# Two 64-feature heads side by side in the value product of a fused attention kernel

## The chip, the cores and the metric

The kernel runs on one core of a Trainium2 chip. The metric is the device time of one execution in microseconds. The engines named below are TensorE (PE; PEld is its weight load), VectorE (DVE), ScalarE (ACT), GpSimd (POOL) and SyncE (SP), which issues the loads. The matmul results land in eight PSUM banks of 128 partitions x 512 f32, bank 0 to bank 7.

## The reference

Two blocks over 256 tokens of 1024 features are computed one after the other. The change lies in the first, `first_block`: in layer 0 eight "moba" heads and eight "fox" heads, in layer 1 four "diff" heads and eight sliding-window ("swa") heads, all but diff with 64 features.

```python
proj = h @ w_in_ab[j]                                     # layer 0
qa, ka, va, ga, qb, kb_, vb_, gb, fb = split_cols(proj, AB_SIZES)
qa, ka = rmsnorm(to_heads(qa, 8), ..), rmsnorm(to_heads(ka, 8), ..)
ya = from_heads(moba_attention(qa, ka, to_heads(va, 8), moba_slopes))
yb = from_heads(fox_attention(qb, kb_, to_heads(vb_, 8), log_f))
y = concatenate([ya * silu(ga), yb * silu(gb)], -1)
x = x + y @ w_out_ab[j]
# every head:  p = softmax(masked scores);  out = p @ v        (256 x 256) @ (256 x 64)
# layer 1 likewise with yc (diff), yd (swa): y = concatenate([yc * silu(gc), yd * silu(gd)], -1)
```

The second block (latent attention, cross-attention over a memory, two MLPs, stick-breaking attention) is not touched, but the kernel begins its memory projection ("mem part") inside the first block.

## The kernel before, in words

Each projection is done to f32 accuracy as three fp32r products (`three`, L498 to L500: high weights by high input, low by high, high by low). Weights stream from memory in units of 128 x 2048, which ScalarE casts to `w_hi` (L1425) and VectorE splits to `w_lo` (L1970), two instructions each for a unit. TensorE takes its work in the order in which the code issues it, and so does every other engine; between engines there are only semaphores. A bank may be written again when its last reader has signalled `readN`.

The attention of the first block is written as pairs of heads with projection work as filling (`pairs`). For pair p TensorE does: the scores of heads 2p and 2p+1 (`scores`, L640, banks 4 and 5), then twice, for the heads of the pair before: the transposes of the probabilities (`turn_probs`, L654, three 128 x 128 blocks in bank 6, the mask leaves the fourth out), a fill (a projection unit or part, given by a table with the fill's number), and the values (`values`, L666, bank 7). VectorE makes the logits and their row maxima (`logits`, L2188), ScalarE the exponentials and their sums (`exps`, L1588), ScalarE copies the transposed probabilities to SBUF (`turned_probs`, L1599), and VectorE takes the reciprocal of the sums (L2204) and multiplies the values by it and by the gate, which is already in SBUF as `arena` (`outputs`, L2213).

The values have the transposed probabilities as weights and the 64 columns of v as the moving side: three f32 matmuls a head, which the trace shows as six instructions of 64 columns. The result has tokens on partitions. The output projection wants features there, so the gated values are transposed on TensorE (`gated`, L552, eight 128 x 128 blocks for eight heads), cast by ScalarE to the high part (L1474) and subtracted by VectorE for the low part (L2026).

The gates silu(ga), silu(gb), silu(gd) come from VectorE (`gate_panel`, L2165), which reads the banks of the gate's projection and so frees them. On GpSimd only small work runs in this stage, the position and forget tables (L2711, L2714, L2717).

Of the kernel before, what the change touches and what calls it, by code (L numbers as in the profile page):

```python
# [21 lines left out]
ALU = mybir.AluOpType  # L22
# [6 lines left out]
P = 128  # L29
D = 1024  # L30
S = 256
# [163 lines left out]
def build(nc, A, out):  # L195
# [7 lines left out]
    with ExitStack() as ctx:  # L203
# [76 lines left out]
        norm_ready = sem("norm_ready")  # L280
# [112 lines left out]
        for k in heads:  # L393
            first_map = k["kind"] == "diff" and k["c"] == 0
            turns += not first_map
            outputs += k["kind"] in ("moba", "fox", "swa") or k["kind"] == "diff" and k["c"] == 1
            norms += k["kind"] in ("mla", "xa") or k["kind"] == "diff" and k["c"] == 1
            k.update(turn=turns, output=outputs, norm=norms)
# [57 lines left out]
        GATE_PARTS = ((0, 2, 4, 3), (2, 1, 5, 5), (3, 1, 6, 7))  # L456
# [5 lines left out]
        def _(pe):  # L462
# [180 lines left out]
            def turn_probs(k):  # L643
# [3 lines left out]
                if k["kind"] in ("moba", "fox", "swa", "sb"):  # L647
                    pe.wait_ge(probs_ready, g + 1)
                else:
                    pe.wait_ge(norm_ready, k["norm"])  # L650
# [6 lines left out]
            def values(k):  # L657
# [10 lines left out]
                end(("Y", g), ins, (y_ready, k["output"]))  # L668

# [199 lines left out]
            def pairs(ks, fill):  # L869

                for p in range(len(ks) // 2 + 1):
                    if 2 * p < len(ks):
                        scores(*ks[2 * p:2 * p + 2])
                    for n in range(2):
                        old = ks[2 * p - 2 + n] if p else None
                        if p:
                            turn_probs(old)
                        for f in fill.get(2 * p + n, []):
                            f()
                        if p:  # L880
                            values(old)

            def gated(name, panel, b0, need, first=0, chunks=4):

                return transposes(name, lambda t, c: arena[:, panel, t * PANEL + (first + c) * P:t * PANEL + (first + c + 1) * P],
                                  chunks, lambda t: (y_ready, need), b0)
# [6 lines left out]
            def gate_part(key, panel, n, ks):  # L893

                first, chunks, b0, last = GATE_PARTS[n]
                yr[key, n] = gated((key, n), panel, b0, ks[last]["output"], first, chunks)

            def gate_chunk(key):
# [11 lines left out]
                0: [unit("qb", 0)], 1: [unit("qb", 1)], 2: [unit("kb", 0)], 3: [unit("kb", 1), turn("qb", 4, 1)], 4: [lambda: row_scales(("n", 0), 1), lambda: fgate(r)],  # L910
                5: [unit("vb", 0), turn("kb", 5, 1)], 6: [lambda: tok_unit("vb", 1, decay_cols)], 7: [unit("gb", 0)], 8: [lambda: turn_mem(0, 0, 2), unit("gb", 1)],
                9: [lambda: turn_mem(0, 1, 2)], 10: [mem_part(0, 0)], 11: [mem_part(0, 1)], 12: [lambda: gate("yab0", 3, 0, heads_of("moba")[-1]["output"])],
                13: [mem_part(1, 0)], 14: [mem_part(1, 1)], 15: [half("oab", 0, "yab0", 0)],
                16: [half("oab", 0, "yab0", 1), lambda: gate_part("yab1", 7, 0, heads_of("fox"))],
                17: [half("oab", 1, "yab0", 0), lambda: gate_part("yab1", 7, 1, heads_of("fox"))]})
            half("oab", 1, "yab0", 1)()
            gate_part("yab1", 7, 2, heads_of("fox"))
# [12 lines left out]
            for i in range(5):  # L930
# [13 lines left out]
                0: [mem_part(2, 1), lambda: gate("ycd0", 3, (0, 3), heads_of("diff")[-1]["output"])], 2: [mem_part(3, 0)], 3: [mem_part(3, 1)],  # L944
                4: [half("ocd", 0, "ycd0", 0)], 5: [half("ocd", 0, "ycd0", 1)], 6: [half("ocd", 1, "ycd0", 0, (0, 1))], 7: [half("ocd", 1, "ycd0", 0, (2, 3))],
                8: [half("ocd", 1, "ycd0", 1, (0,)), lambda: gate_part("ycd1", 6, 0, heads_of("swa"))],
                9: [half("ocd", 1, "ycd0", 1, (1,)), lambda: gate_part("ycd1", 6, 1, heads_of("swa"))]})
            half("ocd", 1, "ycd0", 1, (2, 3))()
            gate_part("ycd1", 6, 2, heads_of("swa"))
# [423 lines left out]
        def read_of(name):  # L1373
# [3 lines left out]
        panel_of = {"qa": 0, "ka": 1, "va": 2, "ga": 3, "qb": 4, "kb": 5, "vb": 6, "gb": 7,  # L1377
                    "qc": 0, "kc": 1, "vc": 2, "gc": 3, "qd": 4, "kvd": 5, "gd": 6}

# [35 lines left out]
        def _(act):  # L1415
# [48 lines left out]
            def hi_one(name, c, dst, base=0, in_bank=2):  # L1464
# [10 lines left out]
                own.sig(ins, hiT_ready)  # L1475

# [187 lines left out]
            def pairs(ks, units_at, after, ahead={}, both_turned=()):  # L1664

                for p in range(len(ks) // 2 + 1):
                    for n in range(2):
                        i = 2 * p + n
                        if p and i - 1 not in both_turned:
                            turned_probs(ks[i - 2])  # L1670
                        if i in both_turned:
                            turned_probs(ks[i - 1])
# [15 lines left out]
            def mem_unit(i, n):  # L1688
# [14 lines left out]
                11: (("xkv", 0, 0), 0), 13: (("xkv", 0, 1), 0), 15: ("oab", 0, 0), 17: ("oab", 1, 0)}, {  # L1703
                0: [lambda: gate_finish("ga")], 1: [qk_squares("qb")], 2: [qk_rsqrt("qb")],
# [4 lines left out]
                12: [lambda: hi_T("yab0", 4, xT_hi)], 14: [lambda: mem_unit(0, 1)],  # L1709
                16: [lambda: hi_T(("yab1", 0), 2, xT_hi, 4)], 17: [lambda: hi_T(("yab1", 1), 1, xT_hi, 6)]},  # L1710
                {9: [lambda: hi_T(("m", 0, 1), 4, hT_hi, 4)], 10: [lambda: gate_finish("gb")]})
            hi_T(("yab1", 2), 1, xT_hi, 7)
# [24 lines left out]
            for i in range(4 + 2):  # L1737
# [22 lines left out]
                for f in extra.get(i, []):  # L1760
                    f()
            pairs(heads_of("swa"), {2: ("gd", 1), 3: (("xkv", 0, 2), 0), 5: (("xkv", 0, 3), 0)},
                  {1: [lambda: hi_T("ycd0", 4, xT_hi)],
                   8: [lambda: hi_T(("ycd1", 0), 2, xT_hi, 4)], 9: [lambda: hi_T(("ycd1", 1), 1, xT_hi, 6)]},
                  {4: [lambda: mem_unit(0, 2), lambda: mem_unit(0, 3)]}, (6,))
            hi_T(("ycd1", 2), 1, xT_hi, 7)
# [194 lines left out]
        def _(dve):  # L1961
# [236 lines left out]
            def recip(k):  # L2198
# [5 lines left out]
                link(V.reciprocal(rsum[:, 2 * g:2 * g + 2], e))  # L2204

            def outputs(k):

                recip(k)
                g, vd = k["g"], k["vd"]
                ps = condition(dve, ("Y", g))  # L2210
# [633 lines left out]
```

## Time and profile before

| quantity | value |
| --- | --- |
| median of 3 runs | 951.78 us (950.68 to 952.01) |
| profiled execution | 951.7 us |
| its span, first to last instruction | 949.9 us |
| TensorE busy | 936.1 us (99%) |
| VectorE busy | 637.9 us (67%) |
| ScalarE busy | 544.1 us (57%) |
| GpSimd busy | 57.2 us (6%) |

The span is what the trace covers; the execution is 1.8 us longer, and the durations below are of the span. The stage of moba and fox lies about at 58 to 157 us, that of swa at 256 to 289 us. In a timeline row "x6" means that six like instructions that follow each other are one row, and its duration is that of the whole row; TensorE's rows overlap by their pipeline, so what a group costs there is the distance from its start to the next start.

### The profile page before, as it was taken

The numbers are of one execution on the slowest core, as the hardware profiler recorded it, in microseconds if no ns is written. First come the engines' busy times: TensorE is split into PE (matmuls) and PEld (weight loads), VectorE is DVE, ScalarE is ACT, GpSimd is POOL, SyncE is SP. The second block draws the span as 40 slices with busy tenths as digits, with TensorE's granted clock in tenths as the row PEclk, the third lists the DMA queues.
The fourth block names the chain that finished last, engine by engine and source line by source line (L and its number), as shares of the span: only waits on it lengthen the run. The fifth ranks groups of instructions, "written<-read, shape, count | busy, mean of one in ns | idle before, by whom it ended". The sixth has DMA issues, their size and how long they took to land.

```text
span 949.9 us, 14440 instructions
## 1 busy us (share of the span) xinstructions
PE 936.1 (99%) x5452; PEld 815.5 (86%) x5452; DVE 637.9 (67%) x1258; ACT 544.1 (57%) x1046; POOL 57.2 (6%) x109
## 2 busy tenths in 40 slices
PE   9999999999999999999999999999999999999997
PEld 7778788888888898989888888899988898888886
DVE  4888784877776667667666656477964767556664
ACT  6686673657676575567444444465754666444442
POOL 3001330002010030000000000000000000000000
PEclk9999999999999999999999999999999999999999
DMA  9986534554334274445556656665455256655641
GB/s 286 260 194 121 175 133 158 181 181 146 136 121 113 77 211 161 149 130 173 187 179 198 200 177 233 183 184 153 139 173 177 89 178 189 204 183 179 201 175 44
DMA packets 109584, 159.88 MB, mean 168 GB/s; under 512 B 10734, under 2 KB 45900, under 8 KB 109260
## 3 DMA queue, kind: packets, MB, share of 16 engines
q1 hardware_dynamic: 109080, 158.40, 53.7%
q8 instruction: 44, 0.72, 0.3%
q10 hardware_dynamic: 436, 0.56, 0.2%
q14 instruction: 24, 0.20, 0.1%
HBM read 156.32 MB, written 2.11 MB: 167 GB/s over the span
## 4 chain that ended last, share of the span: by engine, by line
PE 92%; DVE 3%; ACT 1%; issue 1%; DMA 1%; SPq 1%; DVEq 0%; ACTq 0%
PE bank L498 22%; PE bank L500 22%; PE bank L499 22%; PE bank L1206 9%; PE bank L1209 5%; PE bank L640 3%; PE bank L654 2%; PE bank L666 2%; PE bank L552 2%; DVE w_lo L1970 1%; DMA raw<-in_w_in_ab 1%; PE bank L625 1%; PE bank L1347 1%; SPq L2759 1%; DVE xT L2028 0%
## 5 line engine op out<-in xcount | busy, mean ns | idle before, releaser
L1970 DVE TENSOR_TENSOR w_lo<-raw,w_hi 128x1024 fp32r<-128x1024 f32 (+3 forms) x296 | 335.2, 1177 | 136.6 <-ACT w_hi L1425 136.1
L1425 ACT CAST w_hi<-raw 128x1024 fp32r<-128x1024 f32 (+3 forms) x296 | 282.1, 1011 | 128.2 <-DMA raw<-in_mlp_w_in 72.0
L498 PE MATMUL bank<-w_hi,xT 128*128 128x512 f32 (+1 forms) x366 | 145.2, 397 | 1.4 <-issue 0.9
L500 PE MATMUL bank<-w_hi,xT 128*128 128x512 f32 (+1 forms) x366 | 141.2, 386 | 0.0
L499 PE MATMUL bank<-w_lo,xT 128*128 128x512 f32 (+1 forms) x366 | 140.9, 385 | 0.0
L498 PE MATMUL bank<-w_hi,hT_hi 128*128 128x512 f32 (+1 forms) x348 | 136.7, 393 | 2.0 <-DVE w_lo L1970 1.7
L500 PE MATMUL bank<-w_hi,hT_lo 128*128 128x512 f32 (+1 forms) x348 | 135.0, 388 | 0.0
L499 PE MATMUL bank<-w_lo,hT_hi 128*128 128x512 f32 (+1 forms) x348 | 134.9, 388 | 0.0
L498 PE MATMUL bank<-xT,w_hi 128*128 128x256 f32 x368 | 106.0, 288 | 0.3 <-DVE w_lo L1970 0.3
L1206 PE MATMUL bank<-xT,w_hi 128*128 128x512 f32 x384 | 104.5, 394 | 0.0
L500 PE MATMUL bank<-xT,w_lo 128*128 128x256 f32 x368 | 104.1, 283 | 0.0
L499 PE MATMUL bank<-xT,w_hi 128*128 128x256 f32 x368 | 104.0, 283 | 0.0
L498 PEld LDWEIGHTS bank<-w_hi,xT 128*128 128x128 f32 x366 | 68.8, 188 | 15.5 <-DVE w_lo L1970 2.0
L500 PEld LDWEIGHTS bank<-w_hi,xT 128*128 128x128 f32 x366 | 68.7, 188 | 14.3
L499 PEld LDWEIGHTS bank<-w_lo,xT 128*128 128x128 f32 x366 | 69.0, 188 | 12.3
L498 PEld LDWEIGHTS bank<-w_hi,hT_hi 128*128 128x128 f32 x348 | 65.4, 188 | 16.1 <-DVE w_lo L1970 1.9
L500 PEld LDWEIGHTS bank<-w_hi,hT_lo 128*128 128x128 f32 x348 | 65.3, 188 | 13.6
L499 PEld LDWEIGHTS bank<-w_lo,hT_hi 128*128 128x128 f32 x348 | 65.4, 188 | 12.4
L1206 PEld LDWEIGHTS bank<-xT,w_hi 128*128 128x128 f32 x384 | 66.5, 189 | 9.6
L498 PEld LDWEIGHTS bank<-xT,w_hi 128*128 128x128 f32 x368 | 70.5, 191 | 1.5 <-issue 0.7
L499 PEld LDWEIGHTS bank<-xT,w_hi 128*128 128x128 f32 x368 | 70.5, 192 | 0.3
L500 PEld LDWEIGHTS bank<-xT,w_lo 128*128 128x128 f32 x368 | 70.5, 191 | 0.0
(276 smaller groups left out, 1313.7 us busy)
## 6 DMA issues: line engine op xcount, KB each, us to landing
raw<-in_mlp_w_in SPq DMA_DIRECT2D x32, 1024.0 KB, 5.2
raw<-in_mlp_w_out SPq DMA_DIRECT2D x32, 1024.0 KB, 5.1
raw<-in_w_in_ab SPq DMA_DIRECT2D x13, 1024.0 KB, 10.6
raw<-in_w_in_cd SPq DMA_DIRECT2D x13, 1024.0 KB, 5.1
raw<-in_xa_w_kv SPq DMA_DIRECT2D x8, 1024.0 KB, 5.1
raw<-in_sb_w_qkv SPq DMA_DIRECT2D x16, 512.0 KB, 5.0
raw<-in_w_out_ab SPq DMA_DIRECT2D x4, 1024.0 KB, 5.2
raw<-in_w_out_cd SPq DMA_DIRECT2D x4, 1024.0 KB, 5.1
```

What stands on the lines that cost most here:

```text
L498: pe.matmul(o, wh, ih, start=start, stop=False, skip_group_check=True)
L499: pe.matmul(o, wh, il, start=False, stop=False, skip_group_check=True)
L500: return pe.matmul(o, wl, ih, start=False, stop=stop, skip_group_check=True)
L552: ins = pe.transpose(o, src(t, c), ident[:, :])
L625: ins = pe.transpose(o, arena[:, panel, t * w + c * P:t * w + (c + 1) * P], ident[:, :])
L640: ins = pe.matmul(o[:, a:z], q(t * P, (t + 1) * P), kk(0, z - a), start=n == 0, stop=n == len(k["parts"]) - 1)
L654: ins = pe.transpose(banks[b][:, n * P:(n + 1) * P], src[:, a:a + P], ident[:, :])
L666: ins = pe.matmul(banks[b][:, t * vd:(t + 1) * vd], k["pt"][:, n * P:(n + 1) * P], k["v"](kt), start=m == 0, stop=m == len(mine) - 1)
L1206: pe.matmul(banks[b][:, :], wh[c], xT[:, k].rearrange("p a s -> p (a s)"), start=k == 0, stop=False, skip_group_check=True)
L1209: ins = pe.matmul(banks[b][:, 0:S], wl[c], xT_hi[:, k, :], start=False, stop=k == KC - 1, skip_group_check=True)
L1425: nc.scalar.copy(w_hi[:, u % SLOTS, a], raw[:, u % SLOTS, a]).then_inc(hi_ready, 1)
L1970: V.tensor_tensor(w_lo[:, u % SLOTS, a], raw[:, u % SLOTS, a], w_hi[:, u % SLOTS, a].bitcast(F32), ALU.subtract).then_inc(lo_ready, 1)
```

## The change

The probabilities are divided by their sum before they are transposed, not the values after. For moba this is done by GpSimd (`scale_probs`, two instructions a head, signal `divided`), for fox and swa by VectorE (`normalise`, which the kernel already had for other heads: a reciprocal and two instructions a head, signal `norm_ready`). The values are then done for two heads at once, at the end of the pair: v is the weight (64 columns), the transposed probabilities move, and the two heads stand in the column halves of the array and in the partition halves of bank 7 (`values_pair`). The result has features on partitions, so the output needs no transposes. Instead the gates are transposed (`turn_gate`, eight blocks a gate, into two banks; ScalarE copies the first back to SBUF, VectorE the second), and one VectorE instruction a pair multiplies values by gate (`outputs`). The high and low parts are then made from SBUF (`gated_hi`, `gated_lo`). In the tables of the fills some parts move: the memory parts 1 from 13 and 14 to 12 and 13, the halves of the output projection "oab" from 15 to 17 to 14 to 17, and ScalarE's and VectorE's casts with them.

```diff
 # TensorE
+            def values_pair(ka, kb):
+                begin(("Y", g), 7)
+                pe.wait_ge(probsT_ready, kb["turn"])
+                places = ((ka, 0), (kb, HD))
+                for k, a in places:
+                    pe.matmul(banks[7][a:a + HD, 0:S], k["v"](0), k["pt"][:, 0:S], start=True, stop=False, tile_position=(0, a), ...)
+                for k, a in places:
+                    ins = pe.matmul(banks[7][a:a + HD, P:S], k["v"](1), k["pt"][:, S:S + P], start=False, stop=True, tile_position=(0, a), ...)
+            def turn_gate(name, bs):
+                for t in range(T):
+                    for one in released[name, t]:
+                        pe.wait_ge(*one)
+                for n, b in enumerate(bs):
+                    begin(("gT", name, n), b)
...
+                            ins = pe.transpose(o, arena[:, panel, t * PANEL + c * P:t * PANEL + (c + 1) * P], ident[:, :])
 # pairs, TensorE
                     for n in range(2):
-                        old = ks[2 * p - 2 + n] if p else None
                         if p:
-                            turn_probs(old)
+                            turn_probs(ks[2 * p - 2 + n])
                         for f in fill.get(2 * p + n, []):
                             f()
-                        if p:
-                            values(old)
+                    if p:
+                        values_pair(*ks[2 * p - 2:2 * p])
-                1: [unit("qb", 1)],
+                1: [unit("qb", 1), lambda: turn_gate("ga", (3, 7))],
-                11: [mem_part(0, 1)],
+                11: [mem_part(0, 1), lambda: turn_gate("gb", (0, 1))],
 # swa
-                3: [mem_part(3, 1)],
+                3: [lambda: turn_gate("gd", (0, 3)), mem_part(3, 1)],
 # ScalarE
-                2: [qk_rsqrt("qb")],
+                2: [qk_rsqrt("qb"), lambda: turned_gate("ga")],
-                12: [lambda: hi_T("yab0", 4, xT_hi)], 14: [lambda: mem_unit(0, 1)],
+                12: [..., lambda: turned_gate("gb"), lambda: gated_hi("moba", range(4), 0)],
+                13: [lambda: mem_unit(0, 1)],
 # VectorE
             def outputs(k):
-                recip(k)
...
-                    ins = V.scalar_tensor_tensor(out=o, in0=ps[:, t * vd:(t + 1) * vd], scalar=rsum[...], in1=o, op0=ALU.mult, op1=ALU.mult)
+                own.sig(V.tensor_tensor(o, ps[:, 0:S], o, ALU.mult), gated_ready)
+                        if 2 * p < len(ks) and ks[2 * p]["kind"] == "moba":
+                            recip(ks[2 * p + n], inverted)
+                        elif 2 * p < len(ks):
+                            normalise(ks[2 * p + n])
+                1: [lambda: turned_gate("ga")],
 # GpSimd
+            def scale_probs(k):
+                pool.wait_ge(inverted, g + 1)
+                for t, (a, z) in enumerate(k["spans"]):
+                    ins = G.tensor_scalar(o, o, rsum[:, 2 * g + t:2 * g + t + 1], None, ALU.mult)
+                if n in (3, 5, 7, 9):
+                    scale_probs(heads[n - 3])
+                    scale_probs(heads[n - 2])
```

Three places show how the order changes; each has the rows of the kernel before first. The first is TensorE, after the fill 1 (unit qb 1 into banks 0 and 1), at the scores of heads 2 and 3. "ident" is the identity of the transposes.

```order
L640 MATMUL bank4<-arena 128x128 [waits qkT_ready,logits_ready]
L640 MATMUL bank4<-arena 128x256
L640 MATMUL bank5<-arena 128x128
L640 MATMUL bank5<-arena 128x256
L654 MATMUL bank6<-ident,pb3 128x128 [waits probs_ready,qkT_ready]
L654 MATMUL bank6<-ident,pb3 128x128 x2
L498 MATMUL bank2<-w_hi,xT 128x512 [waits loT_ready,read2,lo_ready]
```

In the changed kernel TensorE has at the same place:

```order
L703 MATMUL bank3<-ident,arena 128x128 [waits read3,read2]
L703 MATMUL bank3<-ident,arena 128x128 x3
L703 MATMUL bank7<-ident,arena 128x128 [waits qkT_ready]
L703 MATMUL bank7<-ident,arena 128x128 x3
L645 MATMUL bank4<-arena 128x128 [waits qkT_ready,logits_ready]
L645 MATMUL bank4<-arena 128x256
L645 MATMUL bank5<-arena 128x128
L645 MATMUL bank5<-arena 128x256
L661 MATMUL bank6<-ident,pb3 128x128 [waits divided,qkT_ready]
L661 MATMUL bank6<-ident,pb3 128x128 x2
L503 MATMUL bank2<-w_hi,xT 128x512 [waits loT_ready,read2,lo_ready]
```

The gate's eight transposes stand ahead of the scores and wait for both halves of gate_panel ga (`read3,read2`, VectorE's L2165). The next rows are the unit kb 0: twelve matmuls into bank 2, then twelve into bank 3. In both kernels the first into bank 3 waits for `read3`; in the kernel before VectorE's L2165 gives it, now ScalarE's copy of the transposed gate. That copy is here, on ScalarE, at head 2; in the kernel before ScalarE has there:

```order
L1588 ACTIVATE pb3,esum<-nl3,nmax 128x128 [waits written6,logits_ready]
L1588 ACTIVATE pb3,esum<-nl3,nmax 128x256
L1425 CAST w_hi<-raw 128x1024 [waits w_in3]
L1425 CAST w_hi<-raw 128x1024
L1460 ACTIVATE lnv<-var 128x16 [waits var_ready]
L1462 ACTIVATE guess<-lnv 128x16 [waits act_chain]
L1599 COPY pt3<-bank6 128x384 [waits written6]
```

And in the changed one:

```order
L1634 ACTIVATE pb3,esum<-nl3,nmax 128x128 [waits written6,logits_ready]
L1634 ACTIVATE pb3,esum<-nl3,nmax 128x256
L1458 CAST w_hi<-raw 128x1024 [waits w_in3]
L1458 CAST w_hi<-raw 128x1024
L1493 ACTIVATE lnv<-var 128x16 [waits var_ready]
L1495 ACTIVATE guess<-lnv 128x16 [waits act_chain]
L1514 COPY arena<-bank3 128x512 [waits written3,written7]
L1645 COPY pt3<-bank6 128x384 [waits written6]
```

The copy (L1514) stands behind the exponentials of head 2, the casts of the next weight unit and two small instructions, and ahead of the copy of head 1's probabilities. The third place is ScalarE at head 12; in the kernel before, with the copies of the probabilities of heads 10 and 11 as first and last row:

```order
L1599 COPY pt3<-bank6 128x384 [waits written7,written6]
L1588 ACTIVATE pb3,esum<-nl3,nmax 128x128 [waits written6,logits_ready]
L1588 ACTIVATE pb3,esum<-nl3,nmax 128x256
L1474 CAST xT<-bank0 128x256 [waits written0] x2
L1474 CAST xT<-bank1 128x256 [waits written1] x2
L1599 COPY pt3<-bank6 128x384 [waits written7,written6]
```

In the changed kernel, between the same two copies:

```order
L1645 COPY pt3<-bank6 128x384 [waits written7,written6]
L1634 ACTIVATE pb3,esum<-nl3,nmax 128x128 [waits written6,logits_ready]
L1634 ACTIVATE pb3,esum<-nl3,nmax 128x256
L1458 CAST w_hi<-raw 128x1024 [waits w_in0]
L1458 CAST w_hi<-raw 128x1024
L1514 COPY arena<-bank0 128x512 [waits written0,written1,units_used]
L1521 CAST xT<-arena 128x256 [waits gated_ready] x4
L1645 COPY pt3<-bank6 128x384 [waits written7,written6]
```

In the kernel before the casts of the next weight unit come behind head 13; now they and the copy of the transposed gate gb (bank 0) stand at head 12, ahead of the four high parts and of the copy of head 11's probabilities, for which the values of the pair (10, 11) wait.

## Rows read from the trace of the kernel before

**Rows 1.** The page: busy time of each engine, and granted TensorE clock in 40 slices.

```profile
PE 936.1 (99%) x5452; PEld 815.5 (86%) x5452; DVE 637.9 (67%) x1258; ACT 544.1 (57%) x1046; POOL 57.2 (6%) x109
...
PEclk9999999999999999999999999999999999999999
```

**Rows 2.** TensorE, timeline: start us, us, engine, line, op, out<-in, count [idle before].

```profile
67.57 0.93 PE L640 MATMUL bank<-arena 64*128 64x128 f32 x8
68.44 0.55 PE L654 MATMUL bank<-ident,pb 128*128 128x128 f32 x3
68.74 0.47 PE L498 MATMUL bank<-w_hi,xT 128*128 128x512 f32 x1
74.29 0.78 PE L666 MATMUL bank<-arena,pt 128*128 128x64 f32 x6
```

**Rows 3.** VectorE and ScalarE, timeline of the same stretch.

```profile
67.71 1.41 DVE L2165 SCALAR_TENSOR_TENSOR arena<-bank,rstd,xn 128x512 f32<-128x512 f32 x2 [0.27 <-ACT xn L1575]
69.59 2.36 DVE L1970 TENSOR_TENSOR w_lo<-raw,w_hi 128x1024 fp32r<-128x1024 f32 x2 [0.47 <-ACT w_hi L1425]
73.39 0.28 DVE L2188 CUSTOM_DVE_ANT_0 nl<-bank,alibi 128x128 f32<-128x128 f32 x1
74.07 0.40 ACT L1588 ACTIVATE pb<-nl,nmax 128x128 f32<-128x128 f32 x1 [2.29 <-DVE nmax L2188]
74.96 1.98 ACT L1425 CAST w_hi<-raw 128x1024 fp32r<-128x1024 f32 x2
```

**Rows 4.** Groups by form: line, engine, op, shapes, count, busy us, mean ns, idle before.

```profile
L666 PE MATMUL bank<-arena,pt 128*128 128x64 f32 x144 | 18.9, 267 | 1.3 <-DVE arena L2213 1.1 <-ACT pt L1599 0.2
L2222 DVE TENSOR_SCALAR pb<-pb,rsum 128x256 f32<-128x256 f32 x8 | 2.8, 349 | 0.0
L2044 DVE COPY mem<-bank 128x512 f32<-128x512 f32 x4 | 2.7, 682 | 0.0
L1696 ACT COPY mem<-bank 128x512 f32<-128x512 f32 x8 | 4.5, 583 | 0.2 <-PE bank L500 0.2
```

**Rows 5.** GpSimd, one group by form.

```profile
L2711 POOL TENSOR_SCALAR alibi<-arena,small 128x256 f32<-128x256 f32 x8 | 7.4, 924 | 0.0
```

**Rows 6.** TensorE, timeline of the cross-attention values.

```profile
406.11 0.60 PE L676 MATMUL bank<-arena,mem 128*128 128x256 f32 x2
406.54 0.59 PE L677 MATMUL bank<-arena,mem 128*128 128x256 f32 x2
```

**Rows 7.** TensorE, timeline around the fox heads' middle.

```profile
126.00 0.88 PE L666 MATMUL bank<-arena,pt 128*128 128x64 f32 x6 [1.08 <-DVE arena L2213]
126.98 0.36 PE L498 MATMUL bank<-hT_hi,w_hi 128*128 128x256 f32 x1
129.93 0.78 PE L666 MATMUL bank<-arena,pt 128*128 128x64 f32 x6
130.64 0.93 PE L640 MATMUL bank<-arena 64*128 64x128 f32 x8
```

**Rows 8.** VectorE and ScalarE, timeline of the same stretch.

```profile
125.28 0.16 DVE L2204 RECIPROCAL rsum<-esum 128x2 f32<-128x2 f32 x1
131.21 2.56 DVE L1970 TENSOR_TENSOR w_lo<-raw,w_hi 128x1024 fp32r<-128x1024 f32 x2
133.69 0.28 DVE L2188 CUSTOM_DVE_ANT_0 nl<-bank,alibi 128x128 f32<-128x128 f32 x1
130.12 1.99 ACT L1425 CAST w_hi<-raw 128x1024 fp32r<-128x1024 f32 x2
135.25 1.17 ACT L1474 CAST xT<-bank 128x256 fp32r<-128x256 f32 x4
136.30 0.51 ACT L1599 COPY pt<-bank 128x384 f32<-128x384 f32 x1
```

**Rows 9.** TensorE and ScalarE, timeline of the sliding-window heads.

```profile
268.90 1.98 ACT L1425 CAST w_hi<-raw 128x1024 fp32r<-128x1024 f32 x2
270.11 0.48 PE L498 MATMUL bank<-w_hi,xT 128*128 128x512 f32 x1
```

More of the change, by code:

```diff
@@ L395, in build @@
             turns += not first_map
-            outputs += k["kind"] in ("moba", "fox", "swa") or k["kind"] == "diff" and k["c"] == 1
-            norms += k["kind"] in ("mla", "xa") or k["kind"] == "diff" and k["c"] == 1
+            outputs += k["kind"] == "diff" and k["c"] == 1
+            norms += k["kind"] in ("fox", "swa", "mla", "xa") or k["kind"] == "diff" and k["c"] == 1
             k.update(turn=turns, output=outputs, norm=norms)
@@ L646, in turn_probs @@
                 begin(("PT", g), b)
-                if k["kind"] in ("moba", "fox", "swa", "sb"):
+                if k["kind"] == "sb":
                     pe.wait_ge(probs_ready, g + 1)
+                elif k["kind"] == "moba":
+                    pe.wait_ge(divided, g + 1)
                 else:
@@ L891, in gate, with gate_chunks @@
                 yr[key] = gated(key, *a)
-            def gate_part(key, panel, n, ks):
-                first, chunks, b0, last = GATE_PARTS[n]
-                yr[key, n] = gated((key, n), panel, b0, ks[last]["output"], first, chunks)
+            def gate_chunks(key, chunks):
+                yr[key] = chunks_ready(state["loT"])
+                state["loT"] += chunks
             def gate_chunk(key):
@@ L1475, in hi_one, with turned_gate, gated_hi @@
                 own.sig(ins, hiT_ready)
+            def turned_gate(name):
+                condition(act, ("gT", name, 1))
+                ps = condition(act, ("gT", name, 0))
+                nc.scalar.copy(pan(panel_of[name], 0), ps[:, :]).then_inc(read_of(("gT", name, 0))[0], 1)
+                own.last = read_of(("gT", name, 0))
+            def gated_hi(kind, ps, base):
+                for p in ps:
+                    act.wait_ge(gated_ready, pair_no[kind] + p + 1)
+                    own.sig(nc.scalar.copy(xT_hi[:, base + p, :], gated_chunk(kind, p)), hiT_ready)
             def hi_T(name, chunks, dst, base=0):
@@ L1662, in _, with pairs @@
             front("qa", "ka", "va", "ga")
-            def pairs(ks, units_at, after, ahead={}, both_turned=()):
+            def pairs(ks, units_at, after, ahead={}):
                 for p in range(len(ks) // 2 + 1):
@@ L2203, in recip, with turned_gate, gated_lo @@
                     link(V.tensor_tensor(e, e, col(ESINK + 2 * k["h"], 2), ALU.add))
-                link(V.reciprocal(rsum[:, 2 * g:2 * g + 2], e))
-            def outputs(k):
-                recip(k)
-                g, vd = k["g"], k["vd"]
-                ps = condition(dve, ("Y", g))
-                for t in range(T):
-                    o = k["gate"](t)
-                    ins = V.scalar_tensor_tensor(out=o, in0=ps[:, t * vd:(t + 1) * vd], scalar=rsum[:, 2 * g + t:2 * g + t + 1],
-                                                 in1=o, op0=ALU.mult, op1=ALU.mult)
-                    own.sig(ins, y_ready if t == T - 1 else None)
+                link(V.reciprocal(rsum[:, 2 * g:2 * g + 2], e), s)
+            def turned_gate(name):
+                ps = condition(dve, ("gT", name, 1))
+                V.tensor_copy(pan(panel_of[name], 1), ps[:, :]).then_inc(read_of(("gT", name, 1))[0], 1)
+                own.last = read_of(("gT", name, 1))
+            def outputs(k):
+                o = gated_chunk(k["kind"], k["h"] // 2)
+                ps = condition(dve, ("Y", k["g"]))
+                dve.wait_ge(*read_of(("gT", {"moba": "ga", "fox": "gb", "swa": "gd"}[k["kind"]], k["h"] // 4)))
+                own.sig(V.tensor_tensor(o, ps[:, 0:S], o, ALU.mult), gated_ready)
+            def gated_lo(kind, ps, base):
+                for p in ps:
+                    dve.wait_ge(hiT_ready, lo_T[0] + 1)
+                    lo(xT_lo[:, base + p, :], gated_chunk(kind, p), xT_hi[:, base + p, :], None)
             def normalise(k):
@@ L2313, in _, with pairs @@
             front("qa", "ka", "va", "ga")
-            def pairs(ks, after, late, between={}, early=()):
+            def pairs(ks, after, late, between={}):
                 for p in range(len(ks) // 2 + 1):
```

103 lines of the change are left out of this document (60 added, 43 removed).

## The prediction

> **What bounds the kernel now.** I read the page first. TensorE is busy for 936.1 us of a span of 949.9 [rows 1], so a microsecond of TensorE work or waiting is a microsecond of time, and work on another engine costs only where TensorE waits for it. The granted clock is in the top tenth in all 40 slices [rows 1]. Then TensorE's groups by form, for the values and for what they wait [rows 4]: L666 with 64 columns is busy for 18.9 us in 144 instructions, with 1.3 us of idle time ahead of them, 1.1 of it behind VectorE's L2213. Last the timelines at three places where the order changes: fill 1 to 2 [rows 2, 3], heads 8 to 13 [rows 7, 8] and swa [rows 9]. There I replayed the changed order by hand, each instruction with the duration of its nearest row. The reader is to see that these stages run with hardly any idle TensorE, while ScalarE and VectorE are only just ahead.
>
> **The values.** Before, the six instructions of a head take from 129.93 to 130.64 when scores follow, 0.71 us [rows 7], and 0.6 ahead of the transposes, where no row-half mode begins; a pair is 1.32 (my rounding of both). The new pair has two matmuls of 256 and two of 128 columns. The nearest row is the scores L640: two heads side by side in row halves, the same columns, eight instructions, from 67.57 to 68.44 or 0.87 [rows 2]. I add 0.1 for the second mode change and take 0.95. Saving: 12 pairs x 0.37 = 4.4 us. The bounds come from the cross-attention values: two instructions of 256 columns start 0.43 apart from the next two [rows 6], so one f32 product of 256 columns is 0.43 and one of 128 half of it. If the column halves run fully side by side the pair is 0.43 + 0.22 = 0.65, and 12 pairs save 8.0. If they run one behind the other it is 1.30, with the same 0.3 of overhead as L640 has over 0.65 it is 1.6, and 12 pairs cost 3.4 more than before. I take L640's value because it has the same shapes. The Trainium skill, TensorEngine Tiling (Array Packing), Key Properties, says that different tiles can run in parallel and that a change of mode drains the engine. L640's 0.87 against 0.65 agrees with both for row halves; no row here shows column halves.
>
> **The transposes.** 24 of gated values go and 24 of gates come (8 for each of ga, gb, gd), the same blocks at about 0.1 each (three take 0.30 [rows 2]): nothing, but those of ga come early, where TensorE then waits anyway; I count them once, at nothing.
>
> **First wait: gate ga.** TensorE is free for the transposes at 67.57 [rows 2], but the gate's panel is written by L2165 from 67.71 to 69.12 [rows 3], which itself waited for ScalarE. Before, nobody on TensorE needed it until bank 2. Cost 69.12 - 67.57 = 1.55. Queued behind are the scores of heads 2 and 3, on which the whole chain of VectorE and ScalarE hangs, but VectorE is busy with w_lo until 71.95 (69.59 + 2.36), so that harms nobody else.
>
> **Second wait: bank 3.** TensorE then has transposes 0.8, scores 0.87, probabilities 0.30 and the twelve products into bank 2, half of 68.74 to 74.29, 2.78 [rows 2]: it is at bank 3 at 69.12 + 4.75 = 73.87. Bank 3 is now freed by ScalarE's copy, behind the exponentials and the casts. VectorE's logits of head 2 began at 73.39 [rows 3]; ahead of them now stand two reciprocals of 0.16 [rows 8] and the copy of bank 7, 0.68 [rows 4]: 1.0 later. Exponentials then at 74.07 + 1.0 = 75.07, done and cast begun 0.89 later at 75.96, cast 1.98 to 77.94 [rows 3], two small 128x16 instructions, by estimate 0.4, and the copy of 128x512, 0.58 [rows 4]: 78.9. The cost is 78.9 - 73.9 = 5.0. It is the largest term and nothing hides it: TensorE has no other work in its order. The 1.55 and 5.0 are 6.5 together. GpSimd's two instructions for head 0 (0.92 and somewhat less [rows 5]) stand ahead of bank 2's products; as TensorE comes 1.55 + 0.8 later than before, and 5 us of waiting follow, up to 5 us of lateness there cost nothing.
>
> **Heads 8 to 13.** Before values of head 8 TensorE waited until 126.00 for L2213, that is for VectorE behind a w_lo that ended at 125.28 [rows 7, 8]. Now the probabilities of head 9 wait for its normalising behind the same w_lo: 0.16 and twice up to 0.35 [rows 4, 8], to 126.1. One wait takes the place of the other: 0. New is the wait of pair (10, 11). Its scores (12, 13) begin 0.5 later than 130.64, with eight transposes of gb (0.8) more and the first values (0.6) less ahead of them and the pair's 0.24 over one head's values: 131.1. From there 0.87 + 0.3 + twice a memory part of 2.95 (126.98 to 129.93 [rows 7]) + 0.3 = 7.4, so TensorE is at the pair at 138.5. On ScalarE: the logits at 133.69 [rows 8] become 134.4 by the copy of bank 1 on VectorE (0.68), exponentials from 135.0 to 135.9, cast 1.9, copy 0.5 (0.58 less its overlap), four high parts 1.1 and the copy of head 11's probabilities 0.5 [rows 8]: 139.9. Cost 1.4. By the same kind of count, the last fox pair waits 0.6 for a copy behind a cast of 1.98 and two high parts (by estimate), and the wait of 0.2 behind L1599 [rows 4] goes.
>
> **Swa.** The first half of the output projection "ocd" begins at 270.11 [rows 9] and needs bank 0; it comes 0.8 later by the transposes of gd and 0.4 sooner by the pair. ScalarE frees the bank only behind the cast of 268.90, which lasts 1.98 and starts some 1.0 later, since VectorE normalises two heads (0.16 + twice up to 0.35 each, less what L2213 took) ahead of the logits: copy done at 268.9 + 1.0 + 1.9 + 0.5 = 272.3. Cost 1.8, less some 0.4 that the first pair has already lost waiting: 1.4 here and 0.4 there, 1.8 in all.
>
> **Sum.** -4.4 + 6.5 + 1.4 + 0.6 - 0.2 + 1.8 = +5.7 on an execution of 951.7, or 957.4. Two waits behind VectorE at about 103 and 121 us stay; TensorE comes later to them by the delay of the front, and I take 0.2 off: 957.2. The median of the runs is 0.1 above the profiled execution, which changes nothing.
>
> **The rivals.** (1) The column halves do not run side by side. For it: no row shows them; against it: the row halves do. A pair of 1.3 in place of 0.95 costs 4.2: 961.4. (2) The other side: the wait for bank 3 does not form, because ScalarE comes to the copy before TensorE comes to the bank; for that its chain would have to be 5.0 shorter, against what [rows 3] show. It decides alone: with the second wait gone the sum is +0.7, and with pairs of 0.65 it is -2.9, or 948.8. Partly for it: the bound of 0.65 is not excluded; but by itself it gives only 953.6. (3) GpSimd is the late one. Its instructions read SBUF, and so does w_lo on VectorE, from both operands. If each of the 16 instructions runs at twice the 0.92 [rows 5], a head takes up to 3.7 instead of 1.8; head 0 is covered, but for the three later pairs one wait of some 0.6 each is possible: 959.0. Against it: between the reciprocal and the transposes there are 2.8 us of a unit. The Trainium skill, SBUF — State Buffer, states a lock between the two engines' shared port, by which one waits for the other's whole instruction when VectorE has two SBUF inputs; a w_lo instruction lasts 1.18 here (2.36 for two [rows 3]), so by it head 0 would be 1.2 to 2.4 late, and the sum stays, since the wait for bank 3 covers that. (4) The granted clock falls after the 5 us without a matmul. The profile of before has no such idle stretch there, and never a lower clock [rows 1]; if the next 3 us of work ran at half speed it would cost some 3: 960.2.
>
> **How the numbers follow.** My forecast, with pairs of 0.65 to 1.1 and waits as worked out within 1.5 us: 0.62, on its own 953.5 to 959.5. Rival 1: 0.12. Rival 2, or a mixture of most of it with fewer of the later waits: 0.12. Rival 3: 0.06. Rival 4: 0.08. A range of 952.6 to 961.6 leaves out the far side of rival 2 and the edges of 1 and 4. A difference of under 0.2% (1.9 us) cannot be told from no change here. Faster takes most of rival 2, 0.07; same takes its rest and the low edge of the forecast, 0.07; slower is 0.86.
>
> **What would show it right or wrong.** TensorE idle for about 1.5 us ahead of the first L703 with VectorE's L2210 as releaser, and for about 5 us ahead of the thirteenth product of kb 0 (L503 into bank 3), with ScalarE's L1514 as releaser; from there all later instructions 7 us later than before, 0.8 of which comes back where the gated values were transposed. L684 and L687 of a pair 0.95 from start to start of the next group. TensorE waiting 1.4 us for L1645 ahead of the pair (10, 11), and for L1514 at the half "ocd". I am wrong if bank 3 comes free before 75 us, if the pairs cost 1.3 or more, or if a low granted clock stands behind the first long wait.

## The result and the profile after

The changed kernel takes 959.3 us (median of 5 runs, 958.73 to 959.58) against 951.17 us before (median of 5, 950.68 to 952.01): a ratio of 1.0081, interval 1.0069 to 1.0092. It is slower by 8 us. The forecast was 957.2, with a range of 952.6 to 961.6.

The page of the changed kernel, to stand against [rows 1]:

```profile
span 957.7 us, 14333 instructions
PE 933.9 (98%) x5404; PEld 806.1 (84%) x5404; DVE 644.8 (67%) x1257; ACT 546.3 (57%) x1049; POOL 76.1 (8%) x125
...
PEclk9999999999999999999999999999999999999999
```

TensorE has 2 us less work and the span is 7.8 longer, so about 10 us more waiting (the 2 us less hold a stretch of low clock, shown below). The tenths of the granted clock say nothing here: a dip of 3 us is too short for a slice of 24. The timeline of TensorE in the front of the stage answers to [rows 2]:

```profile
69.81 1.06 PE L703 MATMUL bank<-ident,arena 128*128 128x128 f32 x8 [1.96 <-DVE arena L2210]
73.39 0.52 PE L661 MATMUL bank<-ident,pb 128*128 128x128 f32 x3 [1.65 <-POOL pb L2760]
73.67 0.47 PE L503 MATMUL bank<-w_hi,xT 128*128 128x512 f32 x1
79.21 0.80 PE L503 MATMUL bank<-w_hi,xT 128*128 128x512 f32 x1 [2.53 <-ACT arena L1514]
```

There are three waits within ten microseconds where there was none: for VectorE's gate panel (1.96), for GpSimd's scaling of head 0 (1.65), and for ScalarE's copy that frees bank 3 (2.53). What stands behind them on the other engines answers to [rows 3]:

```profile
68.26 1.41 DVE L2210 SCALAR_TENSOR_TENSOR arena<-bank,rstd,xn 128x512 f32<-128x512 f32 x2 [0.26 <-ACT xn L1621]
70.14 2.41 DVE L2015 TENSOR_TENSOR w_lo<-raw,w_hi 128x1024 fp32r<-128x1024 f32 x2 [0.27 <-ACT w_hi L1458]
74.17 0.69 DVE L2254 COPY arena<-bank 128x512 f32<-128x512 f32 x1
74.78 0.28 DVE L2233 CUSTOM_DVE_ANT_0 nl<-bank,alibi 128x128 f32<-128x128 f32 x1
76.34 1.98 ACT L1458 CAST w_hi<-raw 128x1024 fp32r<-128x1024 f32 x2
78.59 0.57 ACT L1514 COPY arena<-bank 128x512 f32<-128x512 f32 x1
69.97 3.28 POOL L2760 TENSOR_SCALAR pb<-pb,rsum 128x128 f32<-128x128 f32 x2 [6.10 <-DVE rsum L2249]
74.23 1.50 POOL L2760 TENSOR_SCALAR pb<-pb,rsum 128x128 f32<-128x128 f32 x2 [0.98 <-DVE rsum L2249]
```

The chain predicted for ScalarE is there link by link: logits at 74.78 behind the copy of bank 7, exponentials at 75.45, cast at 76.34, copy at 78.59 (predicted 78.3 to 78.9), TensorE in bank 3 at 79.21. GpSimd's pair of instructions takes 3.28 us at 69.97, beside VectorE's w_lo, and 1.50 at 74.23, where VectorE works from PSUM. After the wait, windows of one microsecond on TensorE (busy, count, granted clock) show this:

```profile
79.00:80.00 1.00, 0.79 (x2) 0.58 0.00 0
80.00:81.00 1.00, 1.00 (x4) 0.50 0.00 0
82.00:83.00 1.00, 1.00 (x5) 0.71 0.00 0
83.00:84.00 1.00, 1.00 (x8) 1.00 0.00 0
```

The clock is at 0.50, the 1.2 GHz level, from 79.2 to 82.6; products then start 0.43 apart and not 0.23, which over these 3.4 us costs 1.7 (the expectations below put it at 1.8). Later waits, in the same columns as the timeline:

```profile
105.06 0.52 PE L661 MATMUL bank<-ident,pb 128*128 128x128 f32 x3 [0.89 <-ACT arena L1606]
134.58 0.52 PE L661 MATMUL bank<-ident,pb 128*128 128x128 f32 x3 [1.25 <-DVE pb L2275]
148.52 0.65 PE L684 MATMUL bank<-pt,arena 128*64 128x256 f32 x4 [1.47 <-ACT pt L1645]
161.39 0.65 PE L684 MATMUL bank<-pt,arena 128*64 128x256 f32 x4 [0.43 <-ACT pt L1645]
280.06 0.47 PE L503 MATMUL bank<-w_hi,xT 128*128 128x512 f32 x1 [1.18 <-DVE w_lo L2015]
279.38 0.58 ACT L1514 COPY arena<-bank 128x512 f32<-128x512 f32 x1
```

The old waits behind VectorE's decay work and the memory's transposes stay, at 112.47 and 130.22. At 280.06 the page names w_lo, but ScalarE's copy of the gate gd out of bank 0 ends at 279.96, 0.1 ahead of TensorE's start, so it is the bank. And this is the pair of values, whose start-to-start distance answers to the 1.32 of two heads before [rows 7]:

```profile
90.42 0.65 PE L684 MATMUL bank<-pt,arena 128*64 128x256 f32 x4
90.90 0.39 PE L687 MATMUL bank<-pt,arena 128*64 128x128 f32 x4
91.22 0.93 PE L645 MATMUL bank<-arena 64*128 64x128 f32 x8
```

From 90.42 to 91.22 it takes 0.80 us.

I added up TensorE's start-to-start distances by group over both traces. Idle time went from 5.5 to 15.5 us (+10.0); projections take 2.8 more, 1.7 of it the low clock; most of the rest is the last product ahead of each new wait, which counts with its whole 0.39 and not with the 0.23 to a next start; the values of the 24 heads went from 15.7 to 9.6 (-6.1); transposes and scores of all kinds +0.9; small rest +0.2. Together +7.8, the difference of the spans.

### The profile page after: what moved, and what is told of

Its sections match the earlier page's. It is cut to its first block, busy times and chain, and to the rows that moved or that the text cites. A ratio compares the mean times of both kernels' runs of the same rounds, so it can differ in the third digit from the quotient of the medians.

```text
span 957.7 us, 14333 instructions
## 1 busy us (share of the span) xinstructions
PE 933.9 (98%) x5404; PEld 806.1 (84%) x5404; DVE 644.8 (67%) x1257; ACT 546.3 (57%) x1049; POOL 76.1 (8%) x125
## 4 chain that ended last, share of the span: by engine, by line
PE 85%; DVE 6%; ACT 5%; issue 2%; DMA 1%; SPq 1%; DVEq 0%; ACTq 0%
PE bank L503 21%; PE bank L505 20%; PE bank L504 20%; PE bank L1242 9%; PE bank L1245 5%; PE bank L645 3%; ACT w_hi L1458 2%; DVE w_lo L2015 2%; PE bank L661 2%; PE bank L557 1%; ACT pb L1634 1%; DMA raw<-in_w_in_ab 1%; PE bank L1383 1%; DVE xT L2073 1%; PE bank L630 1%
```

## The experiments

Eleven kernels were run, each an edit of the changed kernel, in four groups with runs of the kernel before on the same chip (medians of before 951.42 us for a to d, 951.49 for e to h, 951.76 for i, 951.80 for j and k).

**a. Bank 3 freed early.** ScalarE's order at head 2:

```diff
-                2: [qk_rsqrt("qb"), lambda: turned_gate("ga")],
+                2: [qk_rsqrt("qb")],
...
+                {2: [lambda: turned_gate("ga")], 9: ...     # ahead of the exponentials
```

> ScalarE's copy of the transposed gate ga out of bank 3 is moved ahead of the exponentials of head 2. Theory (the bank is the cost): the copy ends at about 75.0 us, TensorE comes to bank 3 at 76.3, so the wait of 2.7 us goes, and with it the 3.4 us at half clock that followed (1.8 us): 959.3 - 4.5 = 954.8. Rival (the wait only moves): ScalarE's exponentials and casts are the limit of this stretch, TensorE waits for head 1's or 2's probabilities instead, and less than 1.5 us is gained: 958 or more.

Measured 954.13 us, ratio 1.0031 (1.0019 to 1.0042): 5.2 under the changed kernel, 0.7 more than expected. The wait for bank 3 is gone. The profiled execution, at 956.35 the slowest of its seven, has TensorE's first two waits at the same places (1.79 and 1.01) and the low clock from 70.2 to 77.0:

```profile
69.07 1.06 PE L703 MATMUL bank<-ident,arena 128*128 128x128 f32 x8 [1.79 <-DVE arena L2210]
72.66 0.87 PE L661 MATMUL bank<-ident,pb 128*128 128x128 f32 x3 [1.01 <-POOL pb L2760]
```

```profile
70.00:71.00 1.00, 1.00 (x9) 0.60 1.01 164
76.00:77.00 1.00, 1.00 (x4) 0.50 0.00 0
```

So the bank is the largest single cause, and the clock can also fall without it, behind the wait for the gate. The mean granted clock is 0.998 in the six other executions and 0.996 in all five of the changed kernel: the 5.2 holds most likely the 1.7 of the low clock as well as the wait.

**b. Moba on VectorE, nothing on GpSimd.** `norms` counts moba too, VectorE calls `normalise` for all heads, and `scale_probs` is gone.

> The moba heads are normalised on VectorE like the others, GpSimd scales nothing. Theory (ScalarE's late copy of bank 3 sets the front, GpSimd's lateness is covered by it): TensorE's wait for head 0's probabilities (1.7 us) goes, but VectorE's logits of head 2 come 1.3 us later by two normalisings of 0.64, the bank with them, so the wait there grows from 2.7 to 5.7; at about 105 us 1.0 is gained. Together about +0.3: 959.6. Rival (GpSimd is itself the cost): both waits for it go and nothing comes in their place, -2.7: 956.6.

Measured 959.22 us, ratio 1.0080 (1.0066 to 1.0094): no gain, as the theory said. The wait for GpSimd is gone, and the products into bank 3 begin 0.84 later than in the changed kernel (80.05 against 79.21):

```profile
70.02 1.92 PE L701 MATMUL bank<-ident,arena 128*128 128x128 f32 x8 [1.96 <-DVE arena L2208]
80.05 0.62 PE L503 MATMUL bank<-w_hi,xT 128*128 128x512 f32 x1 [3.27 <-ACT arena L1512]
```

The wait there is 3.27, not the 5.7 of the theory. A part of the difference is that TensorE came later: its clock was low from 70.0 to 73.5 already, and a second time from 80.3 to 83.7. The first of the two stretches lies ahead of the wait for the bank and is covered by it.

**c. TensorE kept busy ahead of bank 3.**

```diff
+                    if name == "kb" and n == 0 and (t, c) == (1, 0):
+                        keep_busy()          # 24 transposes of ident into bank 6
```

> 24 transposes of the identity into the free bank 6 are put ahead of the wait for bank 3 (extra work, no result is used); at 0.11 us each they fill 2.6 of the 2.7 us of waiting. Theory (the lower clock from 79.2 to 82.6 us comes from that idle time): the granted clock stays 1.00 and the 1.8 us go: 957.5. Rival (the clock falls for the waits before it, or whatever TensorE does there): 959.3 to 959.5, with the same stretch at 0.50.

Measured 957.76 us (956.68 to 959.48 in five), ratio 1.0067 (1.0055 to 1.0080). It does not settle the question: in the profiled execution (959.48) the low clock lies ahead of the filled stretch, from 70.6 to 77.4, behind the wait for the gate. Over the five runs the mean granted clock goes with the time: 0.995 in the two of 959.1 and 959.5, 0.998 to 0.999 in those of 956.7 to 957.8. But this doesn't price the clock alone, since the fill has a fixed length: in the profiled execution TensorE came late to it, and the 24 transposes ran from 78.34 to 80.88, past the 79.2 at which the bank had come free in the changed kernel. Nor is the fill shown to keep the clock up: d, whose order is that of the changed kernel up to its first values at 88.8, has 0.998 in three of its five executions without any fill. By which wait the clock is set off stays open; the last section has a pattern.

**d. One head after the other.** The two loops of `values_pair` become one, so the products of the first head are issued ahead of those of the second.

> In the pair of values the two products of one head are issued one after the other, then those of the other head, where they alternated between the column halves. Theory (the two halves run side by side only where neighbouring instructions are of different halves): a pair goes from 0.80 to about 1.35 us, 12 pairs cost 6.6 us: 965.9. Rival (the overlap does not hang on the order, or there is none and 0.80 is something else): 0.80 stays, 959.3.

Measured 958.55 us, ratio 1.0070 (1.0057 to 1.0082). The rival held:

```profile
88.84 0.66 PE L684 MATMUL bank<-pt,arena 128*64 128x256 f32 x4
89.33 0.40 PE L686 MATMUL bank<-pt,arena 128*64 128x128 f32 x4
89.65 0.93 PE L645 MATMUL bank<-arena 64*128 64x128 f32 x8
```

The pair still takes 0.81. L684 is the product of 256 columns and L686 that of 128. They were issued as 256, 128 for the first head and then 256, 128 for the second, yet the trace has all four instructions of 256 first: the second head's did not wait for the first head's.

The profiled execution of d (957.93) also prices the clock. Its low stretch, from 71.3 to 78.2, lies ahead of bank 3, and TensorE comes to the bank late:

```profile
79.19 0.50 PE L503 MATMUL bank<-w_hi,xT 128*128 128x512 f32 x1 [0.32 <-ACT arena L1513]
```

The products there begin at the same time as in the changed kernel (79.21) but run at the full clock, and the span is 1.6 shorter (956.1 against 957.7). So low clock ahead of the wait costs next to nothing, and behind it, here, about what it takes from the products. The other four runs don't follow the clock: 958.55 at 0.996, 958.76, 959.24 and 956.69 at 0.998.

**h. Both heads in one half.**

```diff
                 for k, a in places:
-                    pe.matmul(banks[7][a:a + HD, 0:S], ...
+                    x, a = a // HD * S, 0
+                    pe.matmul(banks[7][a:a + HD, x:x + S], ...     # the 128 columns likewise
```

> Both heads of a pair are put into the same column half and the same partitions of bank 7, one head in columns 0 to 255, the other in 256 to 511; the gated values of half the heads are then not computed, and what VectorE reads for them is left over. Theory (0.80 for a pair rests on the halves running at the same time): the pair is 1.30 + 0.15 = 1.45 us, +7.8 for 12 pairs, of which waits take back 1 to 2: 965 to 967. Rival (an instruction with 64 weight columns is simply quicker): 0.80 stays, 959.3.

This version leaves out the gated values of half the heads. Measured 963.75 us, ratio 1.0125 (1.0112 to 1.0139), 4.5 over the changed kernel. The pair is 1.45, as the theory has it:

```profile
90.08 1.08 PE L685 MATMUL bank<-pt,arena 128*64 128x256 f32 x4
91.00 0.60 PE L689 MATMUL bank<-pt,arena 128*64 128x128 f32 x4
91.53 0.93 PE L645 MATMUL bank<-arena 64*128 64x128 f32 x8
```

Twelve pairs cost 7.7 more, but the time rose by 4.5: the wait at head 4 (0.9) is gone, and those of the pair (10, 11), of swa and of head 9 are 0.6, 0.6 and 0.2 shorter. All idle time is 2.9 less, so another 0.5 lies in small waits; some 0.4 I can't assign. So 0.80 rests on the two halves working at once.

**e. The front without its waits.** The reciprocals of heads 0 and 4 early, the gate ga transposed in fill 3 into the score banks:

```diff
-                1: [unit("qb", 1), lambda: turn_gate("ga", (3, 7))], ... 3: [unit("kb", 1), ...
+                1: [unit("qb", 1)], ... 3: [lambda: turn_gate("ga", (4, 5)), unit("kb", 1), ...
 # VectorE
+                0: [lambda: settle_head(first_heads[0]), split_to("qb", 0), lambda: gate_panel("ga")],
+                4: [lambda: settle_head(first_heads[4]), fox_z_],
```

> The front of the changed kernel without its waits: head 0's reciprocal is taken ahead of the w_lo of unit qb 0 and head 4's ahead of the forget gate's work, so that GpSimd can scale earlier, and the gate ga is transposed in fill 3 into the score banks 4 and 5 and not in fill 1 into 3 and 7, with ScalarE's copy behind the probabilities of head 1 and VectorE's behind the logits of head 3. Theory (the front's waits and the low clock behind them are 2.1 + 1.7 + 2.7 + 1.8 us, and 1.0 at 105 us): all 9.3 go: 950.0. Rival (banks 4 and 5 only move the wait, to the logits of heads 2 and 3 before and the scores of 4 and 5 behind): at least 2 us stay, 952 or more.

Measured 952.10 us, ratio 1.0002 (0.9993 to 1.0011): 7.2 of the 9.3 us go. By its number the rival held (952 or more), but not by its mechanism: no wait has moved to banks 4 and 5. The profile shows a clock of 1.00 throughout the stretch and two waits, both for GpSimd:

```profile
68.58 0.52 PE L661 MATMUL bank<-ident,pb 128*128 128x128 f32 x3 [0.20 <-POOL pb L2768]
75.41 0.52 PE L661 MATMUL bank<-ident,pb 128*128 128x128 f32 x3 [0.84 <-POOL pb L2768]
```

**f. The later waits alone.** VectorE normalises head 9 ahead of a w_lo; ScalarE copies the probabilities of heads 11 and 15 ahead of gate and high parts, and the gate gd ahead of an exponential.

> Only the later waits are treated: head 9 is normalised ahead of the w_lo of unit gb 1; ScalarE copies the probabilities of head 11 before the gate gb and the four high parts, those of head 15 before two high parts, and the gate gd ahead of the exponentials of the third swa head. Theory (these are waits of order and nothing else): 1.4, 1.6, 0.6 and 1.3 us go but for 0.6 in all: 959.3 - 4.3 = 955.0. Rival (ScalarE is full there, the copies that now come later are waited for instead): less than 2 us gained, 957.3 or more.

Measured 957.64 us, ratio 1.0070 (1.0057 to 1.0084): the rival held, 1.7 gained.

```profile
136.69 0.65 PE L684 MATMUL bank<-pt,arena 128*64 128x256 f32 x4 [0.56 <-ACT pt L1645]
146.45 0.65 PE L684 MATMUL bank<-pt,arena 128*64 128x256 f32 x4 [1.49 <-DVE arena L2263]
155.31 0.65 PE L684 MATMUL bank<-pt,arena 128*64 128x256 f32 x4 [0.54 <-ACT pt L1645]
289.36 0.65 PE L684 MATMUL bank<-pt,arena 128*64 128x256 f32 x4 [1.10 <-ACT pt L1645]
```

The treated waits, 1.25 + 1.47 + 0.43 + 1.18, are 4.3 in the changed kernel and 3.7 here, and the wait for the gate ga, untreated, is 0.9 shorter in this execution. Of the treated ones each is met one or two places further on, three of them at a copy of probabilities, which stands behind the exponentials of a head whose logits are late, and one (146.45) because VectorE's product with the gate now waits for ScalarE's later copy of gb.

**g. Both together.**

> Both sets of reorderings together. Theory (waits add up, and what stays is the saving of the values, 0.52 a pair, and of the two old waits): 959.3 - 9.3 - 4.3 = 945.7, faster than the kernel before by 5.5. Rival (with the early waits gone TensorE runs ahead of VectorE and ScalarE, and the later waits grow): 948 or more.

Measured 950.85 us, ratio 0.9992 (0.9984 to 1.0001): not to be told from the kernel before. The rival held; the later waits are those of f.

**i. g and the copies in a third order.** ScalarE's pairs get a list of heads at which both copies of probabilities stand ahead of the exponentials (10, 14 and swa 6), the gate gb and the high parts move to head 12, and GpSimd scales head 6 ahead of the forget tables.

> Both sets of reorderings (g), and in addition: ScalarE copies the second head's probabilities of the pairs (8, 9), (12, 13) and swa (4, 5) ahead of the exponentials of the next head, takes the copy of the gate gb and the four high parts ahead of the exponentials of head 12, and GpSimd scales head 6 ahead of the forget tables. Theory (TensorE's waits in g of 0.56 + 1.50 + 0.54 + 1.10 + 0.66 us are each for an instruction that stands behind one that waits itself): at least 3.5 of the 4.4 us go: 950.9 - 3.5 = 947.3 or less, faster than the kernel before. Rival (the copies now wait for TensorE and hold the exponentials up): under 1.5 gained, 949.4 or more.

Measured 950.24 us, ratio 0.9987 (0.9978 to 0.9996), the only version that is faster than the kernel before, by 0.13%, within the 0.2% that I had called the limit of what can be told, though its interval lies below 1. Only 0.6 was gained over g, where the theory had 3.5: here too the waits moved.

```profile
129.32 1.06 PE L703 MATMUL bank<-ident,arena 128*128 128x128 f32 x8 [1.25 <-DVE arena L2213]
130.85 0.65 PE L684 MATMUL bank<-pt,arena 128*64 128x256 f32 x4 [0.46 <-DVE arena L2265]
139.91 0.65 PE L684 MATMUL bank<-pt,arena 128*64 128x256 f32 x4 [0.78 <-ACT pt L1645]
```

**j. Only the reciprocals of e.**

> Of e only the two reciprocals: those of heads 0 and 4 are taken earlier on VectorE, so that GpSimd scales the two heads earlier; the gate ga stays in fill 1 and bank 3 is freed as late as in the changed kernel. Theory (GpSimd's lateness at head 0 lies inside the wait for bank 3): TensorE's 1.7 us ahead of head 0's transposes go, the wait for bank 3 grows from 2.7 to 4.4, and only the 1.0 us at head 4 is gained: 958.3, with the low clock where it falls. Rival (the two waits are separate costs): 956.6.

Measured 958.69 us, ratio 1.0075 (1.0061 to 1.0088). The theory held in the trace: the wait for GpSimd at head 0 is gone and that for bank 3 is 4.17 in place of 2.53.

```profile
69.95 1.06 PE L703 MATMUL bank<-ident,arena 128*128 128x128 f32 x8 [1.96 <-DVE arena L2210]
79.30 0.79 PE L503 MATMUL bank<-w_hi,xT 128*128 128x512 f32 x1 [4.17 <-ACT arena L1514]
```

**k. The reciprocals and the early bank.**

> The early reciprocals of j and the early copy out of bank 3 of a. Theory (with both causes gone only the wait for the gate is left in the front, 2.1 us, and the clock stays high behind so short an idle time): 954.1 - 1.3 (head 0) - 1.0 (head 4) = 951.8. Rival (the low clock comes from the wait for the gate alone): 1 to 1.5 us more, with a stretch below 1.00 behind 70 us.

Measured 952.17 us (951.39 to 954.25 in eleven), ratio 1.0007 (0.9998 to 1.0016): the theory's 951.8 on the median. The profiled execution is the slowest, 954.25, and has the rival's dip behind the wait for the gate:

```profile
70.00:71.00 1.00, 0.93 (x7) 0.80 1.13 178
73.00:74.00 1.00, 1.00 (x6) 0.50 1.14 168
```

The dip is not all of the spread: one execution has 953.56 at a mean clock of 0.999.

a, j and k together show how the two causes of the front hang together: taking GpSimd's lateness away gains 0.6 alone, the bank 5.2 alone, both 7.1. The wait for the gate adds little to them. The median of k is that of e (952.17 and 952.10), although k keeps this wait (1.92 at 70.07) and e has none; by the means of the eleven executions each, 952.7 and 951.7, it is worth 1.0. The two waits for GpSimd in e, 0.20 and 0.84, are not in k: they stand in the gate's place.

## Why the prediction was right, and where it was not

**The direction and the front: right.** The wait for bank 3 is the step on which the forecast stood, and a and j show it. I had counted 1.55 for the gate and 5.0 for the bank with GpSimd's lateness inside; the trace has 1.96 of idle time for the gate, since everything on ScalarE and VectorE came 0.5 later than in the profile of before (L2210 at 68.26, not 67.71), and 1.65 + 2.53 = 4.2 for the other two. That GpSimd's lateness at head 0 costs nothing as long as the bank is late is what j measured. As an idle time, though, the bank's wait is 2.53 and not 5.0; GpSimd's stands in front of it and takes 1.65 of the same stretch.

**The values: mis-sized.** I took 0.95 for a pair and it is 0.80; the saving is 6.1, not 4.4. The nearest row, L640's 0.87, was the scores, and I added 0.1 for a second mode change. That was counted twice: the distances between L640's own starts (0.21 for the first product, where 128 columns take 0.11, and 0.32 for the last, where 256 take 0.21) already hold a break at the entry and one at the exit. The pair of values has smaller ones in all, 0.27 for 0.22 at the entry and 0.21 for 0.11 at the exit. The mechanism, two halves at once, is shown by d and h, and rival 1 fell.

**The clock: a rival came true beside the forecast.** I gave 0.08 to the low clock and priced it at 3; it took 1.7 in the changed kernel's profiled execution, behind a wait of 2.53 and not of 5. A low clock behind the first long wait was one of my three signs of being wrong, and it came. It was wrong to treat it as another case, since it adds to the waits and does not replace them. I had also tied it to the longest wait; a, b, c, d and k show dips that begin behind the first one. And "never a lower clock" was read off slices too coarse for it. The trace of before has 0.50 from 945.7 us to its end, behind TensorE's last product, where it costs nothing:

```profile
946.00:947.00 1.00, 0.00 (x0) 0.50 0.00 0
```

**GpSimd at head 4: missed.** The wait of 0.89 at 105.06 is put down by the page to ScalarE's L1606, but GpSimd's row of 101.30 explains it, and its group by tile, from 69 to 106 us, shows why:

```profile
101.30 3.61 POOL L2760 TENSOR_SCALAR pb<-pb,rsum 128x128 f32<-128x128 f32 x2 [0.64 <-DVE rsum L2249]
L2760 POOL TENSOR_SCALAR pb<-pb,rsum x11: 602/922/3031, 70.0 to 105.8; 128x128 f32<-128x128 f32 x6, 128x256 f32<-128x256 f32 x5
```

The scaling ended at 104.91, 0.15 ahead of TensorE's start. In j, with head 4's reciprocal earlier, the wait is gone, and 0.62 of it comes back at head 6. Of rival 3 this much was true; its other places did not show. The durations are 0.60 and 0.92 us undisturbed and up to 3.03 beside w_lo. The Trainium skill, SBUF — State Buffer, Summary: rules for kernel authors, says that when VectorE's instruction has two SBUF inputs and GpSimd's reads SBUF, the second one to issue is blocked until the first finishes. The trace agrees in kind, but the delay, 1.8 to 2.1 us a pair of scalings, is nearly as long as two w_lo instructions back to back (2.4), which one instruction (1.2) does not give.

**Heads 8 to 13 and swa: right in place and nearly in size.** Predicted: the old wait replaced one for one (1.08 before, 1.25 now), 1.4 at the pair (10, 11), 0.6 at the last fox pair, 1.4 + 0.4 in swa. Measured idle: 1.47, 0.43, 1.18 + 0.14. What I had not seen is how little they are worth treating: f took the causes away that I had named, and 3.7 of the 4.3 us came back at the next place.

**The sum.** 957.2, with 1.7 more saved in the values, 0.4 more at the gate, 0.8 less at head 0 and the bank, 0.9 at head 4, 1.7 for the clock, 0.5 less in the later waits, and 1.1 more for the breaks in the stream of products (0.16 at each of some seven new waits), which I had left out: 958.3. The remaining 1.0 to the median is about the growth of transposes and scores that the account above has. That the forecast came within 2.1 us is in part luck: 3.0 of these errors point one way and 5.1 the other.

## What to carry to other kernels

When a buffer's reader changes engine, ask what stands ahead of the new reader in its own order: the copy of 0.6 us that frees bank 3 was late because a cast of 2 us and an exponential that itself waited stood in front of it. A saving on the engine that bounds the kernel (6.1 us) is lost when the new hand-overs put that engine behind engines that were only just ahead; and waits of this kind are not a list to be struck off, since behind each stands the next at nearly the same distance.

## What the runs showed of the hardware

- Products in the two column halves of the array ran at the same time and did not wait for each other's order: 0.80 and 0.81 us for two heads of 256 + 128 columns in f32 in the two orders of issue, 1.45 in the same half.
- In nine of the kernels (the changed one, a, b, c, d, f, h, j, k) the granted clock fell to 0.50 for stretches of 3.4 to 6.8 us, from 0.1 ahead of to 1.5 us behind the end of a wait of TensorE of 1.8 to 4.2 us. Not every such wait had a fall behind it (1.96 at 69.81 in the changed kernel had none), and it was not always the same wait in kernels that differ only later on. It went with the start of the execution, where TensorE's 128x128 transposes begin 0.21 us apart and then 0.11, though the profile gives no lower clock there: where this change came at 5.2 to 6.5 us (a, b, c, d, k) the first fall is behind the gate, where it came at 7.5 to 7.7 (the changed kernel, f, h, j) it is behind bank 3. That is a pattern of nine executions and no experiment; what sets the fall off stays open. In e, g, i and the kernel before no wait was longer than 1.7 us and the clock fell only behind TensorE's last product.
- GpSimd's scaling from SBUF took 0.60 us for 128x128 and 0.92 for 128x256 alone. One that began just behind the first of two w_lo instructions of VectorE took 2.69 (128x128) and 2.70 and 3.03 (128x256). The w_lo instructions took 1.21 to 1.27 as ever, also the one at 70.14 that began while a scaling ran.
